# Compact chunk matrices in the delta branch of a fused two-block kernel, its decay made earlier, its sums of squares by TensorE, and steps of the second block placed anew

## The reference, cut to what matters

```python
def chunk_gated_delta_rule(q, k, v, beta, g):      # 4 heads of 128, 256 tokens, chunks of C = 64
    ...
    gc = jnp.cumsum(g..., axis=-1)                  # within a chunk
    diff = gc[..., :, None] - gc[..., None, :]
    decay = jnp.exp(jnp.where(incl, diff, -jnp.inf))
    kk = jnp.einsum('bhntd,bhnjd->bhntj', kc, kc)
    L = jnp.where(strict, bc[..., :, None] * kk * decay, 0.0)
    rhs = jnp.concatenate([kc * (bc * jnp.exp(gc))[..., None], vc * bc[..., None]], axis=-1)
    sol = lax.linalg.triangular_solve(L + jnp.eye(C), rhs, left_side=True, lower=True, unit_diagonal=True)
    W, U0 = sol[..., :DK], sol[..., DK:]
    A_qk = jnp.einsum('bhntd,bhnjd->bhntj', qc, kc) * decay
    ...
    def step(state, xs):                            # over the 4 chunks
        U = U0_n - W_n @ state
        o = qg_n @ state + A_n @ U
        new_state = ge_n * state + ke_n.T @ U
```

## Time and profile before

| | |
|---|---|
| runs (us) | 1451.27, 1457.21, 1450.38 |
| profiled execution (us) | 1457.47 |
| its span, first to last instruction (us) | 1455.2 |
| mean granted TensorE clock | 0.983 |
| TensorE busy with matmuls | 1387.3 us, 95% |
| VectorE busy | 1087.9 us, 75% |
| ScalarE busy | 757.7 us, 52% |
| GpSimd busy | 65.5 us, 5% |
| HBM | 153 GB/s over the span |

### The profile page before, as it was taken

One profiled execution on the slowest core, in us unless ns is written; L12 is line 12 of the kernel. 1 busy time (PEld: TensorE's weight loads), 2 busy tenths in 40 slices (PEclk: granted clock), 3 DMA queues, 4 the chain that ended last, 5 costly groups with the idle time before them and its releaser, 6 DMA issues.

```text
span 1455.2 us, 25617 instructions
## 1 busy us (share of the span) xinstructions
PE 1387.3 (95%) x10286; PEld 1304.2 (90%) x10286; DVE 1087.9 (75%) x1900; ACT 757.7 (52%) x1209; POOL 65.5 (5%) x58
## 2 busy tenths in 40 slices
PE   7999999999999999999999999999987999988998
PEld 6899999989999888999999899998877898977996
DVE  6899897767677669998977687666698547697446
ACT  6544646546444455445565554445663345754343
POOL 0000000000000000000000000000012100012100
PEclk9999999999999999999999999999999999998999
DMA  8555345554655646553555555655531114430112
GB/s 278 178 191 192 124 146 174 190 192 169 203 189 173 217 153 203 174 174 103 187 169 180 173 199 179 202 161 189 169 116 30 59 59 146 158 120 21 59 59 102
DMA packets 108846, 224.05 MB, mean 154 GB/s; under 512 B 6036, under 2 KB 17556, under 8 KB 108600
## 3 DMA queue, kind: packets, MB, share of 16 engines
q1 hardware_dynamic: 106352, 219.06, 45.5%
q10 hardware_dynamic: 2376, 3.35, 0.7%
HBM read 221.34 MB, written 1.06 MB: 153 GB/s over the span
## 4 chain that ended last, share of the span: by engine, by line
PE 37%; DVE 9%; ACT 3%; issue 2%; DMA 1%; POOL 0%; ACTq 0%; DVEq 0%; POOLq 0%
PE bank L480 12%; PE bank L489 6%; PE bank L455 6%; PE bank L502 5%; PE bank L510 2%; DVE wlo L1721 2%; DVE w L2248 2%; PE bank L460 1%; PE bank L525 1%; PE bank L1103 1%; PE bank L1106 1%; ACT whi L1135 1%; DVE w L2245 1%; DVE w L2261 1%; PE bank L1008 0%
## 5 line engine op out<-in xcount | busy, mean ns | idle before, releaser
L1721 DVE TENSOR_TENSOR wlo<-ring,whi 128x1024 fp32r<-128x1024 f32 (+3 forms) x430 | 497.7, 1178 | 180.8 <-ACT whi L1135 153.1
L1135 ACT ACTIVATE whi<-ring 128x1024 fp32r<-128x1024 f32 (+3 forms) x430 | 433.0, 1026 | 361.7 <-PE bank L480 225.7
L480 PE MATMUL bank<-hhi,whi 128*128 128x256 f32 x2016 | 282.1, 282 | 6.8 <-ACT sgb L1393 4.8
L489 PE MATMUL bank<-hhi,wlo 128*128 128x256 f32 x2016 | 282.3, 282 | 0.0
L480 PE MATMUL bank<-hlo,whi 128*128 128x256 f32 x2016 | 276.2, 279 | 0.0
L480 PEld LDWEIGHTS bank<-hhi,whi 128*128 128x128 f32 x2016 | 255.6, 190 | 10.4 <-ACT sgb L1393 5.5
L489 PEld LDWEIGHTS bank<-hhi,wlo 128*128 128x128 f32 x2016 | 254.6, 190 | 2.9 <-issue 2.3
L480 PEld LDWEIGHTS bank<-hlo,whi 128*128 128x128 f32 x2016 | 252.8, 189 | 0.0
L455 PE MATMUL bank<-w 128*128 128x128 f32 (+6 forms) x880 | 132.5, 303 | 12.9 <-ACT w L1527 4.5
L455 PEld LDWEIGHTS bank<-w 128*128 128x128 f32 (+2 forms) x880 | 114.3, 196 | 22.3 <-issue 8.9
L1899 DVE SCALAR_TENSOR_TENSOR w<-w,par 128x256 f32<-128x256 f32 x240 | 98.0, 477 | 0.0
(11 more groups left out here) (306 smaller groups left out, 1641.2 us busy)
## 6 DMA issues: line engine op xcount, KB each, us to landing
ring<-in_w_in SPq DMA_DIRECT2D x100, 1024.0 KB, 5.1
ring<-in_w_ffn_down SPq DMA_DIRECT2D x22, 1024.0 KB, 4.9
ring<-in_w_ffn_gate SPq DMA_DIRECT2D x20, 1024.0 KB, 5.0
ring<-in_w_ffn_up SPq DMA_DIRECT2D x20, 1024.0 KB, 5.1
ring<-in_w_merge SPq DMA_DIRECT2D x8, 1024.0 KB, 5.0
ring<-in_w_out SPq DMA_DIRECT2D x8, 1024.0 KB, 5.2
ring<-in_w_oc SPq DMA_DIRECT2D x4, 1024.0 KB, 5.2
ring<-in_w_od SPq DMA_DIRECT2D x4, 1024.0 KB, 5.1
```

What stands on the lines that cost most here:

```text
L480: done = e.matmul(o, wh[:, k, cols(u)], s_[:, k0 + k, :], stop=False, skip_group_check=True, start=opens and k == 0 and s_ is sh and u % 2 ...
L489: done = e.matmul(o, wl[:, k, cols(u)], sh[:, k0 + k, :], start=False, stop=closes, skip_group_check=True)
L1135: e.activation(part_of(whi, j), part_raw(j), ACT.Copy).then_inc(*up("hi.a"))
L1721: e.tensor_tensor(part_of(wlo, j), part_raw(j), part_of(whi, j), ALU.subtract).then_inc(*up("lo.v"))
```

## The change

The matrices of the delta branch are stored with 64 columns a head and chunk, the two chunks of a block in the two halves of the partitions. All passes over them shrink from 128x1024 to 128x512, or from 128x512 to 128x256 for a block. The products become twice as many, each of 64 rows by 64 columns, in two halves of the rows and of PSUM's partitions. The decay is one addition, one subtraction and one exponential over 128x512 and becomes a third step of `decay`; the masks `tri` and `strict` go, and a constant `ahead` stands for them. `rs` is multiplied in once (`Dr`), ahead of both scores. The squares of `kc` and `qc` are taken on ScalarE from SBUF, and TensorE sums them over the channels by a product with a column of ones. `kc` is turned later, at the new step 5. `BT` has two buffers, so GpSimd masks a level one level ahead. The plans are new; in the first block's plan six steps of `conv` and six of `indexer` move by 1 or 2 places.

The plans and constants:

```diff
 _at = 0
-for _n, _w in (("ident", 128), ("tri", 128), ("strict", 128), ("lv", 6 * 128),
...
 MIX_PLAN = {
         "tables": [1, 2, 12, 15, 15, 15, 15],
-        "conv": [20, 20, 20, 33, 33, 33, 43, 45, 47, 47, 52, 52, 52, 55, 58, 62, 63, 91, 95, 99, 106, 112, 112, 117,
+        "conv": [19, 19, 19, 32, 35, 35, 43, 45, 47, 47, 52, 52, 52, 55, 58, 62, 63, 91, 95, 99, 106, 112, 112, 117,
...
 TWO_PLAN = {
-        "bias": [4, 4, 6, 16],
-        "taps": [14, 14, 22, 23, 35, 39],
-        "others": [30, 33, 44, 46, 46, 47],
-        "decay": [10, 15],
-        "delta": [21, 22, 25, 25, 28, 34, 37, 38, 39, 40, 46, 46, 46, 46, 46, 46, 47, 49, 50, 51, 52, 53, 55, 63, 67],
-        "latent": [27, 32, 32, 32, 35, 37, 39, 41, 42, 42, 54, 58, 66],
-        "outs": [61, 66, 70, 72],
+        "bias": [5, 6, 6, 21],
+        "taps": [15, 15, 22, 26, 35, 35],
+        "others": [26, 30, 43, 46, 46, 47],
+        "decay": [10, 20, 22],
+        "delta": [21, 23, 24, 24, 24, 34, 37, 38, 39, 40, 42, 42, 42, 44, 46, 46, 47, 49, 50, 51, 53, 54, 55, 60, 67],
+        "latent": [28, 32, 32, 32, 35, 37, 39, 41, 44, 44, 54, 58, 63],
+        "outs": [61, 64, 70, 70],
 }

```

TensorE:

```diff
+            def spread(bk, v):
+
+                for tb in range(2):
+                    for h in range(4):
+                        for hf in range(2):
+                            r = chunk_rows(hf)
+                            done = group(bk[r, c64(4 * tb + h)], [(v[r, tb, h:h + 1].to_broadcast([64, 64]), ident[r, r])])
+                return done
...
+                yield 2
+                bk = ps.take(e, "s", "gcT", l)
+                e.wait_ge(*at("edl", "in", l))
+                spread(bk, gc).then_inc(*up("decay.p"))
+                put("decay.p", "gcT", l)
...
+            def squares_p(name, l, sq, tag):
+                bk = ps.take(e, "s", tag, "sums", l)
+                for h in range(4):
+                    if h % 2 == 0:
+                        e.wait_ge(*at(tag, "squares", l, h // 2))
+                    for tb in range(2):
+                        done = group(bk[:, tb * 4 + h:tb * 4 + h + 1], [(sq[:, h, cols(tb)], onesb[:, 0:1])])
+                done.then_inc(*up(name))
+                put(name, tag, "sums", l)
...
+            def scores_p(name, l, src, tag):
+                bk = ps.take(e, "s", tag, "scores", l)
+                for tb in range(2):
                     for h in range(4):
-                        done = turn(bk[:, cols(h)], src[:, h, cols(tb)])
-                    done.then_inc(*up(name))
-                    put(name, tag, "turned", l, tb)
-
-            def scores_p(name, l, tb, src, tag):
-                bk = ps.take(e, "s", tag, "scores", l, tb)
+                        for hf in range(2):
+                            t = slice(tb * P + 64 * hf, tb * P + 64 * hf + 64)
+                            done = group(bk[chunk_rows(hf), c64(4 * tb + h)], [(kc[:, h, t], src[:, h, t])])
+                done.then_inc(*up(name))
+                put(name, tag, "scores", l)
+
+            def products(bk, left, right):
+
                 for h in range(4):
-                    done = group(bk[:, cols(h)], [(kc[:, h, cols(tb)], src[:, h, cols(tb)])])
-                done.then_inc(*up(name))
-                put(name, tag, "scores", l, tb)
+                    for hf in range(2):
+                        r = chunk_rows(hf)
+                        done = group(bk[r, c64(h)], [(left[r, c64(h)], right[r, c64(h)])])
+                return done
```

Here `delta` on TensorE, from step 0 to the chunks:

```diff
             def delta_p(l):
                 yield 0
-                turned_p("delta.p", l, kc, "kc")
+                squares_p("delta.p", l, ksq, "kc")
+                yield 1
+                scores_p("delta.p", l, kc, "L")
                 yield 2
+                bk = ps.take(e, "s", "r1T", l)
                 e.wait_ge(*at("r1", l))
-                for tb in range(2):
-                    bk = ps.take(e, "s", "gcT", l, tb)
+                spread(bk, r1).then_inc(*up("delta.p"))
+                put("delta.p", "r1T", l)
+                yield 4
+                bk = ps.take(e, "s", "BT0", l)
+                e.wait_ge(*at("BT", l, 0, 0))
+                for g in range(8):
+                    for hf in range(2):
+                        r = chunk_rows(hf)
+                        done = group(bk[r, c64(g)], [(BTs[0][r, c64(g)], ident[r, r])])
+                done.then_inc(*up("delta.p"))
+                put("delta.p", "BT0", l)
+                yield 5
...
                     yield 4 + 2 * lv
                     for tb in range(2):
                         bk = ps.take(e, "s", "M", l, lv, tb)
                         e.wait_ge(*at("BT", l, lv, tb))
                         e.wait_ge(*at("T", l, lv - 1, tb))
-                        for h in range(4):
-                            done = group(bk[:, cols(h)], [(BT[tb][:, cols(h)], T_[tb][:, cols(h)])])
-                        done.then_inc(*up("delta.p"))
+                        products(bk, BT[lv % 2][tb], T_[tb]).then_inc(*up("delta.p"))
                         put("delta.p", "M", l, lv, tb)
...
                     for tb in range(2):
                         bk = ps.take(e, "s", "MT", l, lv, tb)
                         e.wait_ge(*at("M", "in", l, lv, tb))
                         e.wait_ge(*at("TT", l, lv - 1, tb))
-                        for h in range(4):
-                            done = group(bk[:, cols(h)], [(Mm[tb][:, cols(h)], TT[tb][:, cols(h)])])
-                        done.then_inc(*up("delta.p"))
+                        products(bk, Mm[tb], TT[tb]).then_inc(*up("delta.p"))
                         put("delta.p", "MT", l, lv, tb)
...
+                            products(bk, TT[tb], Mm[tb]).then_inc(*up("delta.p"))
                             put("delta.p", "TM", l, lv, tb)
...
+                bks = [ps.take(e, "s", "W", l, hf) for hf in range(2)]
+                e.wait_ge(*at("ktk", l))
+                for tb in range(2):
                     e.wait_ge(*at("TT", l, 5, tb))
                     for h in range(4):
-                        done = group(bk[:, cols(h)], [(ktk[:, tb, cols(h)], TT[tb][:, cols(h)])])
-                    done.then_inc(*up("delta.p"))
-                    put("delta.p", "W", l, tb)
+                        for hf in range(2):
+                            r = chunk_rows(hf)
+                            done = group(bks[hf][:, c64(4 * tb + h)], [(ktk[r, tb, cols(h)], TT[tb][r, c64(h)])])
+                            if tb and h == 3:
+                                done.then_inc(*up("delta.p"))
...
                     for h in range(4):
-                        pairs = [(TT[tb][:, cols(h)], vb[:, tb, cols(h)])]
+                        pairs = [(TT[tb][rows, c64(h)], vb[rows, tb, cols(h)])]
                         if c:
-                            pairs.append((WT[:, h, cols(tb)], Sst[h]))
-                        done = group(bk[:, cols(h)], pairs)
+                            pairs.append((WT[:, h, tc], Sst[h]))
+                        done = group(bk[rows, cols(h)], pairs)
                     done.then_inc(*up("delta.p"))
```

ScalarE, VectorE and GpSimd:

```diff
+                yield 2
+                e.wait_ge(*at("Dm", "in", l))
+                e.activation(Dm, Dm, ACT.Exp).then_inc(*up("decay.a"))
+                put("decay.a", "Dm", l)
...
+            def squares_a(name, l, src, dst, tag):
+                for p_ in range(2):
+                    e.wait_ge(*at(tag, "half", l, p_))
+                    e.activation(dst[:, 2 * p_:2 * p_ + 2], src[:, 2 * p_:2 * p_ + 2], ACT.Square).then_inc(*up(name))
+                    put(name, tag, "squares", l, p_)
...
-                        e.activation(Mm[tb], bk[:, :], ACT.Copy).then_inc(*up("delta.a"))
+                            e.wait_ge(*at("qc", "sums", l))
+                        e.activation(Mm[tb], bk[:, 0:256], ACT.Copy).then_inc(*up("delta.a"))
...
+                yield 2
+                tbh = [P, 8, 64]
+                e.tensor_tensor(by_head(Dr), bc(tflat(gc), tbh, 2), bc(con("ahead"), tbh), ALU.add).then_inc(*up(name))
+                e.wait_ge(*at("gcT", l))
+                e.wait_ge(*now(name))
+                e.tensor_tensor(Dm, bank("gcT", l)[:, :], Dr, ALU.subtract).then_inc(*up(name))
+                leave(name, "gcT", l)
+                put(name, "Dm", "in", l)
...
-                for tb in range(2):
-                    scores_v(name, l, tb, "A", AT, Dm)
-                    put(name, "A", l, tb)
+                e.wait_ge(*at("A", "scores", l))
+                e.wait_ge(*at("Dr", l))
+                e.tensor_tensor(AT, bank("A", "scores", l)[:, :], Dr, ALU.mult).then_inc(*up(name))
+                leave(name, "A", "scores", l)
...
+                e.wait_ge(*at("kc", "sums", l))
+                e.tensor_scalar(tflat(ss[:, 0]), bank("kc", "sums", l)[:, 0:8], 1e-6, None, ALU.add).then_inc(*up(name))
+                leave(name, "kc", "sums", l)
                 put(name, "kss", l)
                 yield 1
```

(63 more changed lines are left out.)

134 lines of the change are left out of this document (42 added, 92 removed).

## The result

The changed kernel takes 1471.03 us (median of 20 executions, 1454.93 to 1489.03), the kernel before 1456.25 us in the same runs (median of 20). The ratio is 1.0062, interval 1.0031 to 1.0092. It leaves out every execution more than 1.5% above the fastest of its kernel, and so four of these 20; the medians alone differ by 1.0%. I had forecast 1442 us and faster by more than 0.5%: it became slower, and the time lies above the range. Some 5 us of the distance are the base, for the sum started from the median of the first three runs (1451.27).

A forecast was written before the change was run, and what follows sets the result against it. VectorE paces each block-2 layer until about 1324, then TensorE. Early stretch 0, places 37 to 41 -4, levels -2.0 -1.6 -0.7, W and U +0.2 +3.5: -4.6 a layer, twice -9.2, from 1451.27 to 1442 us; range 1425 to 1466.

The forecast's parts named there:

- (f): U's products as 64x64 and 128x64 tiles: 24 tile-shape changes at 0.14 us, +3.5 us a layer, bounds 0.1 and 5.0.
- rival 3: Waits at places 21, 24 and 26 cost +4 us a layer more, stops lowering the clock: 1450, no change; chance 0.20.
- The early stretch, taken as 0: Up to the first level (place 37), VectorE's savings and the new order's waits about even: 0 us, bounds -8 and +5.
- (a): Sums of squares: TensorE gains 32 instructions and loses 8 turns of `qc`, net +2.7 us a layer; no ScalarE gain taken.
- (b): Spreads of `gc` and `r1` and turn of level 0: +1.0 us a layer on TensorE; scores A and L: -0.3.
- (d): Levels' products at 0.028 us an instruction: 26.1 us become 12.6, +2.4 for tile changes; places 42, 44, 46: -2.0, -1.6, -0.7.
- rival 2: The two array quarters don't run side by side: +7 us a layer, 1465 us, slower; chance 0.20.
- -8.3: Places 37 to 41, softmax chain earlier: -4 us a layer; places 42 to 46, the levels: -2.0, -1.6, -0.7.
- The outputs, taken as dense either way: Outs at the layer's end: dense either way, their projections take what they took.

The follow-up runs named there:

- T first: Changed kernel with the four products with T first and the four with W behind them in each chunk of U: 1466.09 us, ratio 1.0017.
- sums at 15: Changed kernel with the step that forms the gate's sums back from place 20 to place 15: 1483.84 us.
- the best kernel: Changed kernel with full tiles in W and U and the gate's sums back at place 15: 1447.52 us, ratio 0.9922.

## Why the prediction was wrong

**The step that failed: (f), U "+3.5".** Its working held. A product (two instructions) with its change of tile starts every 0.36 us, against 0.22 with full tiles, so 0.14 a change, and a chunk takes 1170.15 - 1167.27 = 2.88 us as forecast. The first layer's +3.2 is W and U as I had them. What the sum left out is that with these products the clock, once fallen, can stay down for themselves and for all that stands among them: +19.5 in the second layer. First the changed kernel in the layer that held, then in the layer that fell, then the kernel with full tiles:

```profile
1167.27 0.43 PE L467 MATMUL bank<-w 64*64 64x128 f32 x2
1167.62 0.43 PE L467 MATMUL bank<-xn,w 128*64 128x128 f32 x2
...
1170.15 1.10 PE L1029 MATMUL bank<-w,xn 128*128 128x64 f32 x8
```
```profile
1383.23 0.69 PE L467 MATMUL bank<-w 64*64 64x128 f32 x2
1383.85 0.69 PE L467 MATMUL bank<-xn,w 128*64 128x128 f32 x2
...
1388.16 1.97 PE L1029 MATMUL bank<-w,xn 128*128 128x64 f32 x8
```
```profile
1379.43 0.38 PE L468 MATMUL bank<-w 128*128 128x128 f32 x2
1379.65 0.39 PE L468 MATMUL bank<-xn,w 128*128 128x128 f32 x2
```

A long fall costs 17.8 us by the two layers of one execution (65.4 against 47.6) and some 17 by the heaps. At 0.44 a layer that is some 16 us a kernel on average, about as much as the medians differ. The experiment that puts the small tiles into the kernel before shows them sufficient for the long falls, and those that take them out show them needed: of 48 executions one is longer by more than 17 us, the unexplained one at 1472.91.

What the small tiles did to the clock the traces of all thirteen profiled kernels tell more closely. In the stretch of `U` every one of them has a stop of 0.87 us (TensorE waits for VectorE's copy of the first chunk's U), those with full tiles often a second of 0.7. Behind it the clock falls in 16 of the 28 layers profiled, with full tiles too. Here it is in the kernel before, with full tiles:

```profile
1390.93 1.13 PE L455 MATMUL bank<-w 64*128 64x128 f32 x8 [0.75 <-DVE w L2455]
...
1392.70:1396.10 3.40, 3.40 (x17) 3.28 (x17) 1.74 (x4) 1.33 (x2) 0.00 (x0) 0.50 0.00 0
```

The stretches at 0.50 that begin 0.9 to 2.7 us behind such a stop, over both layers of each profiled execution:

```
                                                         layers    with a fall    length, us
full tiles (before, and six changed kernels)               14           7         3.4 each
small tiles for half of U's products                        2           1         3.4
quarters, U's steps apart                                   2           2         3.4 each
quarters, kernel before                                     2           0
quarters, changed kernel (twice), T first, sums at 15       8           6         41.0, one 37.6
```

So the small tiles did not make the clock fall more often than the full ones, as far as so few layers tell; they made a fall of 3.4 us one of some 40. I had weighed the clock in rival 3, as the result of stops. That was right for what stands ahead of a fall, and wrong for its size: how long a fall lasts went with the products that stand behind the stop. Whether the falls would go with the stop of 0.87 us was not tried, for every kernel here has it.

**The early stretch, taken as 0.** Its sizes held too. VectorE's work fell by 60.55 - 51.12 = 9.4 us (forecast 8 and 2). TensorE's own work grew: 68.05 us busy in the best kernel against 65.11, at the same clock of 0.93, where I had (a) and (b) at +3.4. TensorE waited 7.4 us for the squares, where I had some 6 (to 1276 from 1270), 2.4 at place 24 (2 + 2) and 0.9 at 26 (1.5). The error was to hold VectorE's saving against all of this. The passes that VectorE is rid of (decay, scores) come behind this chain and do not shorten it: VectorE came to the gate's sums at 1272.56, and the squares' turn came at 1274.17.

```profile
1269.48 1.28 ACT L1509 ACT_TABLE_LOAD   x1
1272.75 0.17 DVE L2314 TENSOR_TENSOR st<-bank,st 128x8 f32<-128x8 f32 x1
1272.95 0.18 ACT L1509 ACTIVATE st<-bank 128x16 f32<-128x16 f32 x1 [2.19 <-DVE st L2314]
1273.23 1.04 ACT L1168 ACTIVATE whi<-ring 128x1024 fp32r<-128x1024 f32 x1
1274.17 1.14 ACT L1579 ACTIVATE w<-w 128x512 f32<-128x512 f32 x2
1274.94 1.41 PE L467 MATMUL bank<-onesb,w 128*128 128x1 f32 x6 [7.36 <-ACT w L1579]
```

Read upwards: the sums wait for the squares, those for the exponentials of the gate (L1509), and these for VectorE's L2314. That is the chain I had named; with the gate's sums at 15 the early stretch of the second layer is 3.2 us shorter (78.0). Some 1.2 us of TensorE's 69.20 busy are the lower clock itself (0.89; at 0.93 the same work took 68.05). In the first layer the change costs only +2.0, for there the kernel before was the slower one: TensorE stood still for 13.3 us of its early stretch there (2.8 of them in one wait for a load) against 9.7 in the second layer; in the changed kernel it was 10.4 against 12.0.

**The levels, (d): right.** The quarters run side by side.

```profile
1136.99 4.58 PE L467 MATMUL bank<-w 64*64 64x64 f32 x128
...
1144.94 2.08 PE L467 MATMUL bank<-w 64*64 64x64 f32 x64
...
1152.98 1.15 PE L467 MATMUL bank<-w 64*64 64x64 f32 x32
1154.57 1.28 PE L467 MATMUL bank<-w 64*64 64x64 f32 x32 [0.44 <-DVE w L2393]
...
1157.34 2.00 PE L467 MATMUL bank<-w 64*128 64x64 f32 x32
```

128 of them take 4.58 us, (4.58 - 0.27)/127 = 0.034 with the seams between products, and 0.029 within one: 0.028 was right, and rival 2 did not happen. By Gotcha 1 of the Trainium skill's "TensorEngine Tiling (Array Packing)" they should not have run together in one bank (their starts are 0.007 us apart, then 0.05 to the next pair); for two diagonal quarters at different partitions, the measurement decides against it. Levels 3 to 5 take 4.58 + 2.08 + 1.15 + 1.28 and the wait of 0.44, 9.5 us (forecast 10.5, before 15.04). Places 34 to 48 brought -9.8 and -9.1 us against -8.3.

**The outputs, taken as dense either way,** cost 1.4 us a layer more: one part takes 4.8 us in place of 3.3, and in it TensorE waits for VectorE's multiply of `z` by its sigmoid (L2551, 1.4 and 1.3 us in the two layers). The wait is gone with most of the old places back (3.3), but also in the kernel with U's steps apart (3.2), which keeps the new places of `latent` and `outs`. So no one of the moved steps is shown to do it alone.

Without a long fall the two layers come to -2.4 and about 0 (17.5 less the 17.8 of the fall), where I had -4.6 each. The lowest heap therefore equals the kernel before, within 0.5%; rival 3's time, 1450, was near it for half the right reason. By the table and the falls at 0.44 a layer the kernel should be 22 us above the forecast change of -9.2: 16 for the falls, 8 for the early stretch, 3 for the outputs, less 5 for the levels and for `U` without a fall. The medians say 24.

## What to carry to other kernels

A smaller tile does the same work with less of the array. In short bursts between dense products (the levels) that was pure gain; alternating through 30 us it kept TensorE's clock at half, once it had fallen behind a stop of 0.87 us, for some 40 us, in 44% of the layers. Price a small tile by its instructions, its changes of shape, and a lowered clock over everything among which it stands; where the small form saves nothing (here `U` moves as many columns either way), keep the full one. And when a fixed list of places drives several queues, read each engine's queue at the new place before moving a step; and look at the spread of the executions, not at one profile alone.

## What the runs showed of the hardware

- The lower clock was granted to an engine without a gap: 41.00 us busy of 41.00, at 0.50, begun 1.1 us behind a wait of 0.87 us. The eight instructions of L1029 took 1.91 us there in place of 1.04, a product of `U` with its change of tile 0.62 in place of 0.36, a chunk of `U` 4.9 in place of 2.9.
- It comes and goes with the same program: 28 layers of 64 fell for long, and within one execution the first held and the second did not.
- A fall with full tiles, behind the same stop, lasted 3.4 us, in 7 of 14 profiled layers; with the quarters close together 41.0 us (once 37.6), in 6 of 10.
- How the long falls depend on the tiles: full, none in seven profiles, and 47 of 48 executions of the six changed kernels without a step of 17 us; `U`'s W products on half the columns, at most 3 layers of 24; the quarters too, 28 of 64; the same quarters from place 48 to 57 in place of 49 to 53, no steps in six executions.
- A change of tile shape costs 0.14 us between 128x64 and 64x64 (six fewer a chunk gave back 2.88 - 2.03 us), and 0.17 between full tiles and 128x64 (a pair takes 0.78 us in place of 0.44). The Trainium skill has it that changing the tiling mode drains TensorE ("TensorEngine Tiling (Array Packing)", Tiling Modes, Key Properties); that these costs are that drain is not shown here.
